# A hybrid streaming encoder layer on one core: the order of q, k and v in each pair of heads, three score banks with a distance of two, and conv weights rounded block by block

## The reference, cut to what matters

```python
h = _rmsnorm(x, g_mix);  proj = h @ w_in
conv_in = c_gate * u
conv = conv_b + conv_w[2]*padded[:, 2:2+t] + conv_w[0]*padded[:, 0:t] + conv_w[1]*padded[:, 1:1+t]
y_conv = b_gate * conv                                     # 256 channels
q, k = _head_rms(q, gq_fox), _head_rms(k, gk_fox)          # 8 heads of 64
cum = cumsum(concatenate([past_logf, log_sigmoid(f_logit + b_f)]))
y_fox = softmax(q @ k.T / 8 + cum_q - cum_k, causal) @ v   # sample: 128 cached keys first
y_mem = softmax(q_mem @ mem_k.T / 8) @ mem_v               # 4 heads, 256 memory tokens
x = x + concatenate([y_conv, y_fox, y_mem]) @ w_out
```

## Time and profile before

| | us |
|---|---|
| runs, median (range) | 2347.22 (2343.73 to 2347.88) |
| the profiled execution | 2340.95 |
| its span | 2338.9 |
| TensorE busy | 2115.8 (90%) |
| VectorE busy | 1142.1 (49%) |
| ScalarE busy | 780.7 (33%) |
| POOL busy | 347.8 (15%) |
| second fox pair, 1018.00 to 1110.00 | 92.0, TensorE busy 83.95 |
| third fox pair, 1110.10 to 1202.30 | 92.2, TensorE busy 84.03 |

### The profile page before, as it was taken

The page is one execution under the profiler, slowest core; times in us unless marked ns, Lnnn a source line. Parts: engine busy times, 40 slices in busy tenths (PEclk is TensorE's granted clock), DMA queues, the critical chain, the costliest instruction groups (busy, mean ns, idle before and its releaser), DMA issues.

```text
span 2338.9 us, 36837 instructions
## 1 busy us (share of the span) xinstructions
PE 2115.8 (90%) x15188; PEld 1999.8 (86%) x15188; DVE 1142.1 (49%) x1989; ACT 780.7 (33%) x1315; POOL 347.8 (15%) x175
## 2 busy tenths in 40 slices
PE   4599999999999788898898678966999999999996
PEld 4599999999999787785776557955999999999996
DVE  6755556665320242544545645167665656643103
ACT  5332322234221321445445444043222232333213
POOL 0000000005444421101101203000000000044440
PEclk7799999999999898899999888977999999999997
DMA  4522222238532234221220116023222222475222
GB/s 147 138 73 75 74 83 83 79 99 292 165 115 89 97 39 56 68 60 41 56 60 21 46 53 211 1 86 89 83 83 74 90 65 79 134 276 174 91 73 84
DMA packets 214773, 222.16 MB, mean 95 GB/s; under 512 B 27912, under 2 KB 156552, under 8 KB 214096
## 3 DMA queue, kind: packets, MB, share of 16 engines
q1 hardware_dynamic: 214608, 219.81, 31.1%
HBM read 169.98 MB, written 49.80 MB: 94 GB/s over the span
## 4 chain that ended last, share of the span: by engine, by line
PE 83%; DVE 7%; ACT 4%; DMA 3%; issue 2%; SPq 1%; POOL 0%; DVEq 0%; ACTq 0%
PE banks L252 24%; PE banks L253 24%; PE banks L254 24%; PE banks L2109 3%; PE banks L1825 1%; PE banks L2055 1%; PE banks L2095 1%; DMA x_again<-x_spill 1%; PE banks L2096 1%; DMA past_k<-in_cache_fox_k 1%; PE banks L1993 1%; DVE scores_minusF L1682 1%; DVE hforms_lo L1449 1%; DVE hforms_f L1433 1%; ACT q_hi_and_max L1126 1%
## 5 line engine op out<-in xcount | busy, mean ns | idle before, releaser
L252 PE MATMUL banks<-hforms_hi,w_hi 128*128 128x264 f32 x2112 | 604.7, 286 | 65.1 <-DVE hforms_lo L1449 44.4
L253 PE MATMUL banks<-hforms_lo,w_hi 128*128 128x264 f32 x2112 | 606.0, 287 | 0.0
L254 PE MATMUL banks<-hforms_hi,w_lo 128*128 128x264 f32 x2112 | 604.0, 286 | 0.0
L252 PEld LDWEIGHTS banks<-hforms_hi,w_hi 128*128 128x128 f32 x2112 | 402.3, 191 | 68.3 <-issue 35.4
L771 POOL TENSOR_TENSOR w_lo<-w_raw,w_hi 128x1024 fp32r<-128x1024 f32 x88 | 217.9, 2478 | 1387.4 <-ACT w_hi L975 1387.4
L254 PEld LDWEIGHTS banks<-hforms_hi,w_lo 128*128 128x128 f32 x2112 | 401.8, 190 | 0.0
L253 PEld LDWEIGHTS banks<-hforms_lo,w_hi 128*128 128x128 f32 x2112 | 400.9, 190 | 0.0
L254 PE MATMUL banks<-acts_a,w_lo 128*128 128x264 f32 x896 | 256.7, 287 | 0.0
L252 PE MATMUL banks<-acts_a,w_hi 128*128 128x264 f32 x896 | 254.6, 284 | 1.7 <-DVE acts_a L1467 1.7
L253 PE MATMUL banks<-acts_a,w_hi 128*128 128x264 f32 x896 | 255.5, 285 | 0.0
L252 PE MATMUL banks<-h_hi,w_hi 128*128 128x384 f32 (+1 forms) x576 | 199.8, 347 | 22.2 <-DVE h_lo L1301 10.2
(11 more groups left out here) (257 smaller groups left out, 3984.7 us busy)
## 6 DMA issues: line engine op xcount, KB each, us to landing
w_raw<-in_w_ffn_down SPq DMA_DIRECT2D x88, 512.0 KB, 4.3
w_raw<-in_w_ffn_gate SPq DMA_DIRECT2D x48, 512.0 KB, 5.2
w_raw<-in_w_ffn_up SPq DMA_DIRECT2D x48, 512.0 KB, 5.2
act_rows<-act_f SPq DMA_DIRECT2D x44, 528.0 KB, 2.8
acts_f<-act_rows SPq DMA_DIRECT2D x44, 528.0 KB, 5.1
xT<-x_spill SPq DMA_DIRECT2D x3, 4224.0 KB, 16.4
w_raw<-in_w_in SPq DMA_DIRECT2D x20, 512.0 KB, 5.9
x_spill<-xT SPq DMA_DIRECT2D x4, 2112.0 KB, 9.2
```

The lines of the kernel that those rows point to most:

```text
L252: eng.matmul(out, w_hi, x_hi, start=first, stop=False, skip_group_check=added)
L253: eng.matmul(out, w_hi, x_lo, start=False, stop=False, skip_group_check=added)
L254: return eng.matmul(out, w_lo, x_hi, start=False, stop=last, skip_group_check=added)
```

## The change

It reorders and rebinds; it adds no arithmetic.

- `PROJ`: q's three products come ahead of k's, weights with them (`load_mixer`). ScalarE's `q_hi` follows products 2 to 4, VectorE's `q_lo` the norms 1 to 3; `k_twice` and `k_lo` come last, in both kinds.
- `turn_past` goes behind the fifth product (fox) or the fourth (mem), into bank 0.
- `key_blocks`: a new order of the blocks (`FULL`), and the four sample blocks among those of the second head (`SAMPLE_AT`), into banks 7 and 0. Score blocks take banks 2, 3 and 6 in turn (`SBANK`), `weigh(n - 2)` stands behind `keyed(n)`.
- The second head's row-maximum scores all use banks 4+5 (`unit_bank`). Its two turnings both use bank 7, the second behind the copy of the first (`TURN2`).
- `split_in` on POOL also waits for the `k_lo` of the pair before.
- `conv_hi(1)` is issued by block within the first conv step; `forget_log` and `forget_sums` move into the first pair.

```diff
-        PROJ = {"fox": [("k", 0, c) for c in range(3)] + [("q", 1, c) for c in range(3)] +
-                       [("v", 2, c) for c in range(3)],
+        PROJ = {"fox": [(x, b, c) for b, x in enumerate("qkv") for c in range(3)],
+        FULL = {"fox": [(0, 0), (0, 1), (3, 0), (1, 1), (2, 0), (2, 1), (1, 0), (3, 1), (7, 1), (4, 1), (6, 1), (5, 1)],
+                "mem": [(0, 0), (0, 1), (1, 0), (1, 1)]}
+        SAMPLE_AT = {"fox": [2, 5, 8, 9], "mem": [1, 3, 4, 5]}
+            for x, at in enumerate(SAMPLE_AT[kind]):
+                j, e = x % 2, x // 2
+                kc, kr, vo, diag = ends[e]
+                r.insert(n + at, (j, kc, kr, vo, SEQ, DEC, (7, 0)[j], 0, e == 0, e == 1, diag))
-        TURN2 = {"fox": 9, "mem": 3}
+        TURN2 = {"fox": (9, 10), "mem": (3, 3)}
+        SBANK = [2, 3, 6]
+        def unit_bank(n):
+            return 6 if n < 10 and n % 2 == 0 else 4
...
 # POOL, split_in
                     pool.wait_ge(A["proj"], upto(NPROJ, v - ITER["conv"]))
+                    pool.wait_ge(A["kdve"], 4 * (v - ITER["conv"]))
 # ScalarE, conv_step and attend
+                    if it + 1 < ITER["conv"] and p >= 2:
+                        for b in ((), (), (0,), (1, 2))[p]:
+                            conv_hi(it + 1, b)
-                    if n == 1:
+                    if g == 0 and n == 1:
+                        forget_log()
+                    if n == (4 if kind == "fox" else 3):
                         past_keys()
-                    if kind == "fox" and n == 5:
+                    if n in (2, 3, 4):
+                        q_hi(n - 2)
+                    if kind == "fox" and n == 7:
                         k_hi()
-                    if done < 6 and n >= PARTS[kind][done][0] + 2:
+                    if done < 6 and n >= PARTS[kind][done][0] + 3:
                         sum_rough(done)
                         done += 1
-                    if n == TURN2[kind] + (1 if kind == "fox" else 0):
-                        maxima(3)
-                        maxima(4)
+                    for h in range(2):
+                        if n == TURN2[kind][h]:
+                            maxima(3 + h)
 # VectorE, attend
-                for c in range(3):
-                    q_lo(c)
+                    if 1 <= m < 3:
+                        q_lo(m - 1)
+                    if m == 3:
+                        q_lo(2)
+                k_twice()
+                k_lo()
 # TensorE
-                        pe.wait_ge(A["mixed"], 18 * (g - 1) + {0: 3, 1: 6, 4: 9, 5: 12}[b])
+                        pe.wait_ge(A["mixed"], 18 * (g - 1) + {0: 12, 1: 6, 4: 15, 5: 18}[b])
-                        pe.wait_ge(A["smax"], 18 * g + n - 1)
+                        pe.wait_ge(A["smax"], 18 * g + (n - 1 if n < 10 else n))
                     if j:
                         pe.wait_ge(A["smax"], 18 * g + 18)
+                        if h:
+                            pe.wait_ge(A["mcopied"], 5 * g + 4)
-                    if n >= 2:
-                        pe.wait_ge(A["expd"], b0 + n - 1)
-                    at = 512 * (2 + n % 2)
+                    if n >= 3:
+                        pe.wait_ge(A["expd"], b0 + n - 2)
+                    at = 512 * SBANK[n % 3]
+                        if j:
+                            pe.wait_ge(A["mixed"], 18 * g + 3)
-                for n in range(NB[kind] + 1):
+                for n in range(NB[kind] + 2):
                     if n < NB[kind]:
                         keyed(n)
-                    if n:
-                        weigh(n - 1)
+                    if n >= 2:
+                        weigh(n - 2)
```

125 lines of the change are left out of this document (52 added, 73 removed).

## The result

| | before | changed |
|---|---|---|
| runs, median | 2345.66 us | 2309.08 us |
| range | 2343.73 to 2347.88 (4 runs) | 2306.21 to 2311.69 (4 runs) |
| ratio of the two | | 0.9843, 95% interval 0.9826 to 0.9861 |
| span of the profiled execution | 2338.9 us | 2309.6 us |

The kernel is 1.6% faster. The forecast was 2303 us, 6 us too low, and inside its range of 2284 to 2321. Run once more in a later series the changed kernel gave 0.9849 (0.9835 to 0.9862).

The account below looks back on a forecast made before the run. Bound: q's late splitting ends each product stage, then row maxima one by one; key blocks are mostly TensorE work. Savings 21.3 + 6.8 + 2.0 + 14.5 = 44.6 off 2341.0 give 2296.4, plus 6.3: 2303 us, range 2284 to 2321.

Parts of the forecast that it names:

- q ahead of k: Forgetting pairs 2 to 4: first maximum 5.2 us earlier, maxima 1.3 faster at the upper clock, together 6.5 a pair.
- GpSimd's wait: Splitting of the next weights starts about 1 us later at no cost; VectorE's splits get the port alone.
- the 8.5: First memory pair: first maximum at 1329.1 instead of 1337.6, 8.5 us saved between products and first maximum.
- First forgetting pair: Wait for the cached k's DMA goes, minus F comes 2.4 earlier: 6.2 us, plus 0.6 in the loop, 6.8.
- Memory pairs ahead of the loops: Up to the first maximum: 8.5 us saved in the first memory pair, 2.5 in the second.
- The key loops: Fewer exponential waits against shared-bank costs: net 0.6 us saved per forgetting loop, 2.0 and 1.5 in the memory loops.
- rival B: Steadier work keeps TensorE's upper clock in forgetting loops and memory pairs: 12 to 15 us more, 2289 us; chance 0.15.
- 1.6 and 0.9: Forgetting key loops: 1.6 us saved by small sample blocks among large ones, 0.9 by exponential waits gone.
- A: Six key loops cost 2 to 3 us more each through single score bank and ScalarE's order: 2318; chance 0.22 with D.
- the last term: Whole kernel: 6.3 us added because the profiled run before lay that far under its median.
- C: Many short waits in the key loops drop TensorE's clock to 1.2 GHz: slower, up to 2410 us; chance 0.04.
- D: q's copies on ScalarE stall products 0.5 us a chunk, 9 us in all: 2312; counted with A, together 0.22.

Follow-up runs that it names:

- a4: The changed kernel without GpSimd's new wait for the last k remainder: 2318.52 us, 0.9895 of the kernel before.
- a1: The changed kernel with the memory pairs' key loops put back as before the change: 2306.79 us, 0.9846 of the kernel before.
- a3: The changed kernel with the memory pairs' second-head row maxima alternating between banks 5 and 4, and the second turning in bank 5 everywhere: 2294.94 us, ratio 0.9796.
- again: The unedited changed kernel run and profiled once more in a later series: 2307.36 us, 0.9849 of the kernel before.
- b1: The changed kernel with only the second turning of maxima moved to bank 5, without its wait: 2306.35 us, 0.9840 of the kernel before.
- a2: The changed kernel with all key loops, forgetting and memory, put back as before the change: 2308.30 us, 0.9853 of the kernel before.
- b2: The a3 kernel with TensorE's wait for the scaled memory moved behind q's third product in the first memory pair: 2294.94 us, 0.9794 of the kernel before.
- c1: The a3 kernel with key blocks in the old order, key tile by key tile, sample blocks last: 2337.23 us, 0.9970 of the kernel before.
- c2: The a3 kernel at distance one, each block weighed behind the next block's scores: 2310.43 us, 0.9860 of the kernel before.
- c3: The a3 kernel with unread matmuls of constants filling TensorE's waits in the memory pairs: 2290.34 us, 0.9776 of the kernel before.

## Why the prediction was right or wrong

**q ahead of k: right, term by term.** The first maximum comes 5.2 us earlier (forecast 5.2), and the maxima run at the upper clock (1.45 us, forecast 1.3). q's copies at nothing: right, the products take 38.8 for 38.6. k is what is late next, and the chain of its steps ended at 1138.4, 1.1 us behind the products, as worked out.

**GpSimd's wait: right in size, wrong in place.** "Its gain is that VectorE's splits have the port alone" was said with the forgetting pairs, where it is nothing (a4). In the first memory pair it was counted inside the 8.5, by the rows 6.8 us (11.1 for 4.3), and is 6.0 to 7.3.

**First forgetting pair: right in sum** (6.2 to 6.6 for 6.8; 5.3 in a1 and a4, which run the same code there but for GpSimd's wait in a4). Ahead of the loop it is 6.3 to 6.8 for the 6.2 counted, in the loop -0.1 to -0.2 for 0.6. The cached k's wait is gone; the first maximum still waits for minus F:

```profile
963.42 0.31 DVE L1692 CUSTOM_DVE_ANT_0 scores_minusF<-banks,minusF 32x160 f32<-32x160 f32 x1 [4.90 <-DMA minusF<-negF_rows]
```

**Memory pairs ahead of the loops: right** (8.9 and 2.9 for 8.5 and 2.5). The six remainders of q take 3.2 us (1.14, 1.14, 0.94), forecast 3.3. Not foreseen: the second pair's products are 2.4 us shorter; the matmuls are the same and the clock is 0.99 instead of 0.87. The first pair's are 0.3 to 1.6 longer.

**The key loops: the step that failed.** "5.6 less 3.6 to 4.1: net +2.0 and +1.5" for the memory pairs, "net 0.6 saved" for a forgetting pair. (The costs of a memory loop add up to 3.5 to 4.0, a tenth less than the sum written there.) Measured: -1.4 to -5.4, -2.0 to -3.2, and -0.2 with one pair of three at -1.6. The gross gain was partly there: with the banks apart (a3) the loops are 2.8, 2.2 and 0.5 us shorter than before. What was mis-sized is the price of the shared banks. In waits it is what I had (four of 0.52 for the forecast's four steps of 0.6, 0.72 for 0.6, and at bank 0 1.1 us or none for 0.5 to 1). In time it is 4.2 to 8.3 us in the first memory pair and 4.2 to 5.4 in the second. Waits of 2.4 us went and 4.2 or more came back; the rest stands beside a shorter low stretch of the clock. That the waits lengthen that stretch is what the kernels suggest: in the second memory pair it lasts 17.1 us in the four profiles with the single bank (changed, again, a4, b1) and 13.7 in a1, a2, a3, b2, c1 and c2, in the first pair 17.1 to 37.5 with it and 13.7 to 17.1 without, so that a1's 17.1 equals two of the four. The kernel before, whose maxima had their banks apart, had 20.5 and 17.1, behind longer gaps ahead of the maxima. It is not shown: c3, which was to show the clock's part alone, did so for the products and not for the loop. I had charged each wait its length, and counted the clock in rival B, as a gain only. In the forgetting loops the mistake was another: the single bank, charged with 0.65, makes a wait of 0.2 us at most, and the serial turning, charged with 0.8 and 0.5, costs 0.8 (b1), so that the rest of the change there brings 0.5 where I had 1.6 and 0.9. Why so little of these 2.5 came, no run here divides.

**The rivals.** By size A is what happened, and in full. A put 15 us on the loops; they are 12.7 to 15.6 us longer than counted (8.1 to 11.0 in the memory pairs, 4.6 in the forgetting ones). By mechanism it is A's in the memory pairs only, where parting the banks gave back 9.6 to 12.5 us (a3). In the forgetting loops the single bank hardly makes a wait; what was missing there is gain that did not come, and 1.4 us in one loop at a lower clock. The sum gave 2296.4 for a run like the profiled one, and the changed kernel's profiled run took 2311.69, 15 more. The median came out near the forecast because of the last term: I put 6.3 us on for the distance of the profiled run before from its median, and the changed kernel's medians lie 2.6 under the one profiled run and 0.2 over the other. In the three later series the kernel before had medians of 2343.42, 2342.49 and 2344.53 us, 1.5 to 3.6 over the profiled run, so the 6.3 was itself mostly chance. That 2303 lies near 2309 is luck of this kind: two errors of opposite sign. A difference of one draw from its median belongs to that draw and is no term of a sum. Of B, the upper clock under the maxima came, which the forecast held already, and the second memory pair's products gained 2.4 us; a forgetting loop at the upper level throughout was seen once (34.0 us, b1). C did not come: no low stretch inside a forgetting loop is longer than 7 us. Nor did D.

## What to carry to other kernels

When a change takes a PSUM bank for one purpose, list who now shares the others, and whether the wait lies in TensorE's queue in every step; here such waits went with nearly twice their length of time, or more. The cure here was a bank that stood empty for half of the work, because a tile of 256 columns was given two banks made for 1024. An order of blocks is judged by when its output banks come free for the next stage, not only by what covers what (c1: 41 us). And one profile of a stage near the clock's edge is one draw: the same kernel gave 29.7 and 25.6 us for one loop, and I first built a theory on the 29.7.

## What the runs showed of the hardware

- Beside GpSimd's copy and subtraction over 128x1024, VectorE's copy with one SBUF operand was slowed more (0.88 to 3.63 us) than the subtraction with two (0.94 to 3.17); GpSimd's own took 1.2 to 1.3 for 1.04, and 2.4 unchanged (a4 and the changed kernel). Row maxima out of PSUM were not slowed (6.7 us for ten).
- The granted clock fell to 1.2 GHz within a wait of 5.1 us in the first memory pair's products, and did not when 60 matmuls of constants filled all but 1.7 us of it (a3 and c3). Waits of 0.5 us in each of four steps went with a low stretch of 31 and 17 us in two profiles of one kernel, and with 14 us in a3, where they were gone; in a1, without them too, it was 17.
- The same forgetting loop, with the same waits, took 34.0 us at a granted clock of 1.00, 35.4 at 0.95 and 36.9 at 0.91, all in one run (b1).
